# Forget-gate sums and the first key bias moved into the projection, key biases loaded first at even batches, query rounding moved one group ahead

## The reference, cut to what matters

```python
def fox_prompt(q, k, v, logf):
    ct = jnp.cumsum(logf, axis=1).transpose(0, 2, 1)
    ...
        s = jnp.einsum('bqhd,bshd->bhqs', qb, k).astype(jnp.float32) * scale
        s = s + cq[..., None] - ct[:, :, None, :]
        s = jnp.where(kpos[None, :] <= qpos[:, None], s, -jnp.inf)
        p = jax.nn.softmax(s, axis=-1).astype(v.dtype)
    ...
def fox_sample(q, k_new, v_new, lf_new, k_past, v_past, lf_past):
    d_past = lax.cumsum(lp, axis=1, reverse=True) - lp
    c_new = jnp.cumsum(lf_new.astype(jnp.float32), axis=1)
    key_bias = jnp.concatenate([d_past, -c_new], axis=1)
    ...
def reference(...):
    fox_o = fox_prompt(fq, fk, fv, flf)
    dsa_o = dsa_prompt(dq, iq, iw, dk, dv, ik, topk_prompt)
    mix = jnp.concatenate([fox_o, dsa_o], axis=-1) @ w_out[l]
    yp = post_sublayers(yp, mix, ...)
```

## Time and profile before

| | us |
|---|---|
| device time, median of 3 runs | 1556.01 (1555.73 to 1557.89) |
| device time of the profiled execution | 1561.95 |
| its span (first to last instruction) | 1560.1 |
| PE, DVE, ACT, POOL busy in it | 1425.7, 825.9, 673.8, 609.0 |
| mean granted TensorE clock | 0.957 of full |

### The profile page before, as it was taken

How to read it: one execution, slowest core, us unless ns; L and a number is a source line. 1 busy time by engine, 2 the same in 40 slices (tenths; PEclk the granted TensorE clock), 3 DMA queues, 4 the chain that set the end, 5 groups by cost and what they waited for, 6 DMA issues and landing times.

```text
span 1560.1 us, 23323 instructions
## 1 busy us (share of the span) xinstructions
PE 1425.7 (91%) x8976; PEld 1259.2 (81%) x8976; DVE 825.9 (53%) x1613; ACT 673.8 (43%) x1274; POOL 609.0 (39%) x618
## 2 busy tenths in 40 slices
PE   6999989978798598989957999999999999999997
PEld 5869889966676476668847999999999998886885
DVE  3269999758684588844463333333333334114425
ACT  4367878626675488831033222222222333212120
POOL 3421524630222012223345555555555556412041
PEclk9999999988999699979977999999999999999999
DMA  6101222166744131331001221222221236523341
GB/s 218 46 11 56 61 86 76 60 135 149 179 121 135 34 76 42 102 108 55 31 27 55 83 83 68 71 83 82 83 79 64 79 104 222 172 86 108 112 149 54
DMA packets 99710, 141.99 MB, mean 91 GB/s; under 512 B 18328, under 2 KB 76408, under 8 KB 99600
## 3 DMA queue, kind: packets, MB, share of 16 engines
q1 hardware_dynamic: 99600, 140.51, 29.5%
HBM read 106.28 MB, written 24.23 MB: 84 GB/s over the span
## 4 chain that ended last, share of the span: by engine, by line
PE 44%; DVE 2%; POOL 1%; ACT 1%; DMA 1%; issue 1%; POOLq 0%; DVEq 0%; ACTq 0%
PE ffn L2359 28%; PE ffn L2376 5%; PE ffn L2378 5%; PE ffn L2377 5%; DMA down_raw<-in_w_down 1%; POOL h_T_lo L2554 0%; POOL down_lo L2549 0%; DVE rows L1943 0%; DVE rows L1945 0%; DVE h_T_even L2600 0%; POOL w_lo L2527 0%; DVE down_lo L2626 0%; PE ffn L2326 0%; DVE ln_stats L1920 0%; ACT down_hi L2489 0%
## 5 line engine op out<-in xcount | busy, mean ns | idle before, releaser
L2527 POOL TENSOR_TENSOR w_lo<-w_S,w_hi 128x512 fp32r<-128x512 f32 x88 | 120.4, 1368 | 99.6 <-ACT w_hi L2434 99.6
L2359 PE MATMUL ffn<-h_T_hi,w_hi 128*128 128x264 f32 x704 | 143.6, 285 | 0.0
L2359 PE MATMUL ffn<-h_T_lo,w_hi 128*128 128x264 f32 x704 | 143.1, 285 | 0.0
L2359 PE MATMUL ffn<-h_T_hi,w_lo 128*128 128x264 f32 x704 | 142.2, 283 | 0.0
L2376 PE MATMUL ffn<-down_hi,act_hi 128*128 128x512 f32 x352 | 138.4, 393 | 0.4 <-POOL down_lo L2549 0.4
L2378 PE MATMUL ffn<-down_hi,act_lo 128*128 128x512 f32 x352 | 138.3, 393 | 0.0
L2377 PE MATMUL ffn<-down_lo,act_hi 128*128 128x512 f32 x352 | 138.2, 393 | 0.0
L2434 ACT CAST w_hi<-w_S 128x512 fp32r<-128x512 f32 x88 | 54.7, 622 | 180.3 <-PE ffn L2359 179.0
L2549 POOL TENSOR_TENSOR down_lo<-down_raw,down_hi 128x1024 fp32r<-128x1024 f32 x32 | 80.3, 2516 | 108.1 <-ACT down_hi L2489 79.6
L2359 PE MATMUL ffn<-h_B_hi,w_hi 128*128 128x264 f32 x528 | 108.7, 287 | 10.7 <-POOL w_lo L2527 10.7
L2619 DVE TENSOR_TENSOR act_lo<-act_raw,act_hi 128x512 fp32r<-128x512 f32 x44 | 37.5, 856 | 147.4 <-ACT act_hi L2497 147.4
(11 more groups left out here) (360 smaller groups left out, 3959.3 us busy)
## 6 DMA issues: line engine op xcount, KB each, us to landing
down_raw<-in_w_down SPq DMA_DIRECT2D x38, 512.0 KB, 3.8
act<-gated SPq DMA_DIRECT2D x11, 1056.0 KB, 4.2
gate_raw<-in_w_gate SPq DMA_DIRECT2D x11, 1024.0 KB, 5.3
up_raw<-in_w_up SPq DMA_DIRECT2D x11, 1024.0 KB, 5.3
act_raw<-act SPq DMA_DIRECT2D x44, 256.0 KB, 2.8
w_raw<-in_w_in SPq DMA_DIRECT2D x9, 1024.0 KB, 5.5
x_raw<-in_xT SPq DMA_DIRECT2D x8, 528.0 KB, 8.3
key_bias<-scratch_negc SPq DMA_DIRECT2D x8, 512.0 KB, 4.8
```

What stands on the lines that cost most here:

```text
L2359: mm = nc.tensor.matmul(pp[:, bank[to] + ch, 0:PIECE], l, x[name][:, k, ch * PIECE:(ch + 1) * PIECE], start=opens and k == 0 and i == 0, s ...
L2527: nc.gpsimd.tensor_tensor(w_lo[n % 2][:, :, :], weight(m, SCHEME[q][0]), f32(w_hi[n % 2][:, :, :]), ALU.subtract).then_inc(w_lo_done, 1)
```

## The change

In words, part by part:

1. In `project` the last segment's counts go to `w_raw` instead of `pi`. The semaphore `ranked` now steps after segment 5 and after segment 6. PE waits for the first step only and transposes the log gates ahead of its whole last unit. DVE's sums wait for the second. SP loads the cached log gates (`lf_past`) at that point, and, still in `project`, waits for the two stores and loads the bias of head 0. In `fox`, SP first waits for that bias to land.
2. The side work for the sample rows leaves the slots: all of it stands ahead of the first `biased_max`, and `ones` is not needed any more.
3. At even batches the bias is loaded first, ahead of the stacked copies and the value rows.
4. In `dsa` the query groups become `Q_GROUPS` = (1,2), (3,4,5), (6,7), (8). PE and ACT handle a group before the item after which DVE subtracts it.

The core of the diff:

```diff
         def ranks(j):
-            if j % 2 and j > 1:
+            if j % 2 and j > 1 or j == NSEG - 1:
...
+            sp.wait_ge(ranked, 2)
+            sp.dma_start(lf_past[:, :], d["past_logfT"]).then_inc(c["lf_loaded"], 16)
             sp.wait_ge(c_done, 1)
             sp.dma_start(d["negc"], negc[:, :]).then_inc(bias_stored, 16)
             sp.wait_ge(c_done, 2)
             sp.dma_start(d["bias_s"][:, PAST:KEYS_S], bias_new[:, :]).then_inc(bias_stored, 16)
+            sp.wait_ge(bias_stored, 32)
+            sp.dma_start(c["key_bias0"][:, :], d["negc"][0].partition_broadcast(P)).then_inc(c["kb_loaded0"], 16)
...
-            unit(AFTER[-1], range(KD // 2))
             pe.wait_ge(ranked, 1)
             pe.wait_ge(logf_done, 1)
             for t, r0, rows in TILES:
                 mm = nc.tensor.transpose(pi[0:FOX_H, r0:r0 + rows], c["logf"][0:rows, t, :], ident[0:rows, 0:rows])
             mm.then_inc(lfT_done, 1)
-            unit(AFTER[-1], range(KD // 2, KD))
+            unit(AFTER[-1])
...
-                        elif j < NSEG - 1:
+                        elif j < NSEG - 2:
                             did(nc.vector.tensor_scalar(key(j), e, 0.0, -BIG, ALU.is_le, ALU.mult))
                         else:
                             nc.vector.tensor_scalar(key(j), e, 0.0, -BIG, ALU.is_le, ALU.mult).then_inc(ranked, 1)
+            dve.wait_ge(ranked, 2)
...
             if b == 0:
-                sp.wait_ge(bias_stored, 32)
-                load_bias(sp, 0)
+                sp.wait_ge(kb_loaded[0], 16)
                 load_values(sp, 0)
                 load_bias(sp, 1)
-                sp.dma_start(lf_past[:, :], d["past_logfT"]).then_inc(lf_loaded, 16)
...
-                sp.wait_ge(c_done, 3)
+                sp.wait_ge(c_done, 4)
                 sp.dma_start(d["bias_s"][:, 0:PAST], bias_s[:, :]).then_inc(bias_stored, 16)
-            elif b in (2, 6):
+            if b % 2 == 0 and b // 2 + 2 < FOX_H:
+                biased(b // 2)
+                load_bias(sp, b // 2 + 2)
+            if b in (2, 6):
                 stack_head(sp, b + 2 if b == 2 else 6)
...
-            if b % 2 == 0 and b // 2 + 2 < FOX_H:
-                biased(b // 2)
-                load_bias(sp, b // 2 + 2)
...
-        def dve_beside(dve, slot, place):
...
+        def dve_first(dve):
+            nc.vector.memset(q_diag[:, :, :], 0.0).then_inc(start_step, 1)
+            nc.vector.memset(bias_s[:, PAST - 1:PAST], 0.0)
+            nc.vector.tensor_tensor(kT_new[:, :, :], f32(kT_hi[:, :, SEQ:ROWS]), f32(kT_lo[:, :, SEQ:ROWS]), ALU.add)\
+                .then_inc(c_done, 1)
+            dve.wait_ge(start_step, 1)
+            for a in range(4):
                 for r in range(2):
...
             last.then_inc(diag_done, 1)
+            dve.wait_ge(lf_loaded, 16)
+            nc.vector.tensor_tensor_scan(bias_s[:, 0:PAST - 1][:, ::-1], lf_past[:, 1:PAST][:, ::-1],
+                                         lf_past[:, 1:PAST][:, ::-1], 0.0, ALU.add, ALU.bypass).then_inc(c_done, 1)
...
-Q_BETWEEN = {0: (1, 2), 1: (3, 4, 5), 2: (6, 7, 8)}
+Q_GROUPS = [(1, 2), (3, 4, 5), (6, 7), (8,)]
...
             mm.then_inc(k_tr, 1)
+            for n in Q_GROUPS[0]:
+                transpose_q(pe, n)
             pe.wait_ge(k_lo, NT // 2)
             pe.wait_ge(q_lo, 1)
...
         def pe_between(pe, i):
-            for n in Q_BETWEEN.get(i, ()):
-                transpose_q(pe, n)
-            if i == BH - 1:
+            if i < BH - 1:
+                for n in Q_GROUPS[i + 1]:
+                    transpose_q(pe, n)
+            else:
...
             for i in range(2, NT // 2 + 1):
                 round_k(act, i)
+            for n in Q_GROUPS[0]:
+                round_q(act, n)
 
         def act_between(act, i):
-            for n in Q_BETWEEN.get(i, ()):
-                round_q(act, n)
+            if i < BH - 1:
+                for n in Q_GROUPS[i + 1]:
+                    round_q(act, n)
...
         def dve_between(dve, i):
-            for n in Q_BETWEEN.get(i, ()):
+            for n in Q_GROUPS[i]:
                 lower_q(dve, n)
```

## The result

| | before | after |
|---|---|---|
| device time, median | 1556.95 us (1555.73 to 1558.04, 4 runs) | 1543.43 us (1542.35 to 1544.01, 4 runs) |
| ratio | | 0.9909, 95% interval 0.9897 to 0.9921 |
| span of the profiled execution | 1560.1 us | 1542.2 us |
| mean granted clock in it | 0.957 | 0.965 |

The change makes the kernel 13.5 us faster, and I had said 21.9, with 15 to 25.5 as the range. The sign was right, the size was not. The profiled executions differ by 17.9 us, 4.4 more than the medians: part of what I had read in the profile of before belonged to that one execution.

What follows compares the result with a forecast made beforehand. PE was busy 91% of the span, so only stretches where it waits could give: fox's first and fifth pairs, dsa's opening. +0.3 − 5.0 − 8.7 − 8.5 = −21.9 us, from 1556.0 to 1534.1; range 1530.5 to 1541.

Steps and rivals of the forecast that it cites:

- Start of fox: Entry into fox after project: barrier opens 0 to 0.6 us later than before, taken as a loss of 0.3 us.
- The cover for SP's later loads: Start of fox: values, bias 1 and head 1's stack load 3 to 4 us later, costed at nothing.
- First pair: First pair of batches in fox: side work leaves it, −5.0 us, bounds −2.9 and −5.7.
- Opening of dsa: Start of dsa: DVE's three 2.5 us waits for ACT's query rounding go; −8.5 us, bounds −6.5 and −9.
- the +0.4 that I charged for PE's clock: Start of dsa: PE, at its lower clock, delays the second item by some 0.4 us.
- Fifth pair: Fifth pair of batches in fox: the stall for head 5's key bias goes; −8.7 us after a 0.8 charge.
- The excess of 9.5 us: Fifth pair in fox: 25.0 us against 15.5; the 7.7 stall and 1.8 of clock would all go.
- The late chain at 0.8 us: In fox, batch 2's new order blocks SP; 0.8 us charged for one or two small stalls, bounds 0 and 5.
- The late chain takes over: Rival: SP, blocked at batch 2, delays scales, value parts and next biases; 5 us, time 1539, chance 0.16.
- a wait at the first value products: Sign of SP's lateness spreading in fox: PE or DVE waits there in batches 6, 10 or 12.

Runs made afterwards that it cites:

- after_again: The changed kernel, unedited, measured and profiled once more: 1543.72 us, ratio 0.9917 to the kernel before.
- dsa_only: The kernel before with only the query groups of dsa changed: 1549.68 us, ratio 0.9945.
- first_at_6: The changed kernel with the bias first at batch 6 but last again at batch 2: 1541.82 us, ratio 0.9912 to the kernel before.
- ahead_8_10: The changed kernel with the bias last at batch 2, and those of batches 8 and 10 one batch earlier, ahead of the scales load: 1537.23 us, ratio 0.9869.
- part3_only: The kernel before with only the bias loaded first at even batches: 1557.93 us, ratio 1.0010.
- before_again: The kernel before, unedited, profiled in another execution: 1557.53 us, ratio 1.0007.

## Why the prediction was wrong, step by step

**Start of fox (+0.3): right in size, with a cost that was too low and luck that covered it.** The first item entered at 338.68 in after, 338.78 and 338.20 in the two profiles of before. The sum of gates began at 328.78, near the early end of 328.6 to 329.8, the bias was issued at 333.10 (332.9 to 334.1 expected) and PE's first matmul behind the barrier stands at 334.11. The price of `w_raw` was real. These are rows of after: the small operation on `w_raw` for the segment before, then DVE's three for the last segment, then POOL's work beside them:

```profile
318.69 0.16 DVE L934 SCALAR_TENSOR_TENSOR want<-w_raw,most 128x1 f32<-128x1 f32 x1
...
325.30 0.72 DVE L934 SCALAR_TENSOR_TENSOR want<-w_raw,most 32x1 f32<-32x1 f32 x1
326.06 1.31 DVE L937 SCALAR_TENSOR_TENSOR key_buf<-w_raw,want,score 32x1056 bf16<-32x1056 f32 x1
327.40 1.34 DVE L941 TENSOR_SCALAR score<-key_buf 32x1056 f32<-32x1056 bf16 x1
```

```profile
323.12 2.90 POOL L633 TENSOR_TENSOR fox_qT_lo<-stage,fox_qT_hi 128x352 fp32r<-128x352 f32 x1 [2.86 <-ACT fox_qT_hi L473]
326.93 1.25 POOL L633 TENSOR_TENSOR fox_qT_lo<-stage,fox_qT_hi 128x352 fp32r<-128x352 f32 x1 [0.92 <-ACT fox_qT_hi L473]
```

The masking took 1.31, as from `pi`; the small operation 0.72; and the last one 1.34 where before had 0.70: 1.2 us in all. What makes both dear is POOL. The small operation on `w_raw` took 0.16 with POOL idle and 0.72 beside POOL, ending at 326.02 together with POOL's work. The last one took 1.34 with POOL already 0.47 us at work when it began. In before POOL was at work beside it too, but began 0.06 us behind it, at 327.97, and it took 0.70. All thirteen profiles divide in this way: 0.70 in the four with the old front, where POOL began some 0.05 us behind it, and 1.34 or 1.35 in the nine others, where POOL had begun some 0.46 us before it. The rule on POOL's shared interface (the Trainium skill, GPSIMD Engine Reference, Specifications) names DVE instructions of two SBUF inputs; the small operation on `w_raw` is one, and the trace agrees.

The price also reached the barrier. SP was done with the bias at 333.45, later than POOL with its last work (332.91). PE's first matmul behind the barrier stands 1.2 us behind POOL's end in all nine profiles of the new front, and 0.35 us in the four of the old one: 0.8 us, where I had 0.6 as the bound. The first item is no later all the same, because POOL's last work ended at 332.4 to 333.7 in the nine profiles against 333.3 to 334.5 in the four. I had written that POOL's end would not change; no run shows why it did, so the good sum of this term is partly luck. The cover for SP's later loads held.

**First pair (−5.0): right.** −4.9 in after, where the item entered DVE at 354.77 (354.7 expected); 15.51 in after_again is near the other bound.

**Opening of dsa (−8.5): right.** −8.7, the same in every kernel that has it, and whole in dsa_only's time. DVE is full, and the slots' first transposes start at 527.94, 16.1 us after the first item (511.85), as forecast. The waits and the last subtraction alone would be −8.9, so of the +0.4 that I charged for PE's clock some 0.2 came.

**Fifth pair (−8.7): this term failed, in two of its numbers.**

1. *The excess of 9.5 us* was one execution's. Its wait for the bias ended with a DMA whose landing time spreads (9.8 us there, 7.2 to 7.9 in the four other profiles of that order). I wrote that "the gain is compute waits and should carry over" to the median, although that profile lay 5.9 us above it. Of this term alone that was false; by the other profiles the excess is 6.7 to 7.1: 2.5 us less to gain.
2. *The late chain at 0.8 us.* In after pair 4 costs 1.6 and pair 6 3.9 more, 5.5 in all; in after_again 0.4 and 5.9, 6.3 in all. Both are above my upper bound of 5. The chain had two links that I did not price. First, I followed the lateness from batch 2 to the value parts and found 0.8 us of cover left; I named head 4's bias as following the chain, but did not work out its slack. It has 7.0 us between the free buffer and its use, against landing times of 3.5 to 7.4 us in the two profiles of the changed kernel, so 1.9 us in SP's list were enough for a stall. Second, I dismissed later stalls with "in the trace DVE waits for just two of the eight biases": I took a load that nobody waits for as a load with cover. Head 6's was on time because the stall that I removed gave SP 7.7 us to catch up; with the stall gone it too has 7.0 us, and it was issued 4.5 us late.

first_at_6 and ahead_8_10 divide the 5.5 by their profiles: 1.4 to 2.2 came from the block at batch 2, and some 4 from the place of batches 8's and 10's loads behind the scales, which the change did not touch and which had been hidden by the old stall.

**The sum.** −21.9 + 5.5 − 0.8 + 2.5 = −14.7, against −13.5 on the medians. What is left, 1.2, is not explained by a run; it is smaller than what the end of `fox` differs between profiles (35.6 to 38.6 us).

**The rivals.** "The late chain takes over" was the one that came, at 0.16; its price was about right (5 us against 5.5 and 6.3). It had named the next biases too, but the sign by which I wanted to know it, a wait at the first value products, did not come. Its time of 1539 lacked the 2.5 us of the excess. Two errors of one sign went past the range. The range took in each rival alone but no error in the base.

**Open.** part3_only's profile is 1.05 us shorter inside `fox` than before_again's, and its median no better; its first mark is 1.4 us later, with the same instructions ahead of it. I have no run that explains that. Parts 1 and 2, part 3 and part 4, each alone, add up to 13.5 us by their ratios, and the change gives 13.5 on the medians and 14.2 by its ratio. That fits, but the intervals together would allow some 3 us either way.

## What to carry to other kernels

The removed stall had covered other waits, and the new order made one more. When an engine's stall goes, look at every wait that the stall had covered, and give each load its slack: time of use minus the time at which its buffer came free minus its landing. A load that nobody waited for may have been on time only because of the stall. In a queue that is worked off in order, put a load with little slack ahead of any wait for another engine (here 6.2 us), and leave the loads with much slack last: "first everywhere" moved two loads, one of which, by the profiles, only blocked. And before a wait from one profile goes into a sum, see whether that execution lies at the median and whether the wait ends with a DMA.

## What the runs showed of the hardware

- **Landing times spread.** The same 512 KB key bias load took from 3.4 to 9.8 us. In the old order the one for head 5 landed after 7.2 to 9.8 us, behind seven other transfers, and gave waits of 5.37, 5.70, 6.11, 6.26 and 7.74 us in five profiles.
- **The clock after a short gap of PE is not the same from one execution to the next.** Behind the same 2.62 us of idle PE the granted clock fell for some microseconds in ten of twelve profiles and stayed at 1.00 in two; the end of `fox` took 35.6 us where it stayed, and 37.0 to 37.3 or 38.5 to 38.6 where it fell. The two profiles of the kernel before differ by 1.6 us there; its executions beside the experiments spread from 1553.0 to 1560.0 us. With 16 transposes that nobody reads in the gap the clock stayed up, in the one profile taken.
- **Whether POOL is already at work decides the time of some DVE operations.** L941 on 32 rows took 1.34 to 1.35 us in nine profiles, with POOL at work some 0.46 us before it began, and 0.70 in four, with POOL beginning 0.05 us behind it. The small operation on `w_raw` took 0.72 beside POOL and 0.16 with POOL idle; on `pi` it took 0.14 with POOL at work beside it.
